# Where the low parts of a decoder step's weight blocks are made: all on VectorE instead of mostly on GpSimd

## What is computed

```
def mixer_layer(x, ...):                       # twice (DEPTH = 2)
    h = rmsnorm(x, norm_pre)
    p = h @ w_in                               # 1024 x 3840: 30 blocks of 128 columns
    rq, rk, rv, rg, sq, sk, sv, sg, ca, cb, cg = split(p)
    o_r = head_groupnorm(retention(rope(rq), rope(rk), rv)) * silu(rg)
    o_s = stickbreak(sq, sk, sv) * silu(sg)    # z -> log_sigmoid -> cumulative sum -> weights -> @ v
    o_c = conv_module(ca, cb) * silu(cg)       # gate, 31-tap depthwise conv, layernorm, swish, matmul
    y = concat([o_r, o_s, o_c]) @ w_out        # 1024 x 1024: 8 blocks, loaded again for each chunk
    return x + rmsnorm(y, norm_post)
```

## Time and profile before

| | |
|---|---|
| median of 3 runs | 1452.54 us (1452.2 to 1453.28) |
| the profiled execution | 1451.64 us, of which the profile's span is 1449.8 |
| PE busy | 1382.0 us, 95% |
| DVE busy | 891.5 us, 61% |
| ACT busy | 764.6 us, 53% |
| POOL busy | 530.4 us, 37% |
| mean granted TensorE clock | 0.983 of 2.4 GHz |

### The profile page before, as it was taken

The page is one execution under the profiler, slowest core; times in us unless marked ns, Lnnn a source line. Parts: engine busy times, 40 slices in busy tenths (PEclk is TensorE's granted clock), DMA queues, the critical chain, the costliest instruction groups (busy, mean ns, idle before and its releaser), DMA issues.

```text
span 1449.8 us, 22660 instructions
## 1 busy us (share of the span) xinstructions
PE 1382.0 (95%) x8328; PEld 1176.3 (81%) x8328; DVE 891.5 (61%) x1378; ACT 764.6 (53%) x1517; POOL 530.4 (37%) x446
## 2 busy tenths in 40 slices
PE   6999899999999999999999999998999999999996
PEld 4888678778778878899978886886767888789995
DVE  2528998985542455476762398999745235545665
ACT  4555442476435555576645644336754364656642
POOL 1535531444423453131234454234343145431211
PEclk9999999999999999999999999999999999999998
DMA  6212004111023110535342110231111311015353
GB/s 230 73 60 74 20 19 128 59 51 38 15 78 109 54 35 16 164 133 186 120 144 74 44 49 16 63 99 64 36 34 45 98 65 54 16 59 194 130 172 109
DMA packets 81167, 116.99 MB, mean 81 GB/s; under 512 B 17442, under 2 KB 62882, under 8 KB 80930
## 3 DMA queue, kind: packets, MB, share of 16 engines
q1 hardware_dynamic: 65794, 59.98, 13.2%
q10 hardware_dynamic: 15264, 55.58, 11.5%
HBM read 89.81 MB, written 19.23 MB: 75 GB/s over the span
## 4 chain that ended last, share of the span: by engine, by line
PE 74%; DVE 16%; issue 4%; ACT 3%; POOL 1%; DMA 0%; SPq 0%; ACTq 0%; DVEq 0%
PE ring L1051 17%; PE ring L1053 16%; PE ring L1052 16%; DVE MX L1709 6%; PE AV L1202 3%; DVE MX L1710 3%; PE Z L1166 3%; PE Z L1266 2%; DVE MX L1806 2%; PE Z L1182 1%; DVE stop_lo L1584 1%; PE ring L1088 1%; PE ring L1074 1%; PE Z L1196 1%; PE Z L1180 1%
## 5 line engine op out<-in xcount | busy, mean ns | idle before, releaser
L1051 PE MATMUL ring<-H_hi,w_hi 128*128 128x352 f32 x1824 | 608.1, 333 | 13.4 <-DVE H_lo L899 5.4
L1053 PE MATMUL ring<-H_hi,w_lo 128*128 128x352 f32 x1824 | 587.6, 322 | 0.0
L1052 PE MATMUL ring<-H_lo,w_hi 128*128 128x352 f32 x1824 | 586.9, 322 | 0.0
L1051 PEld LDWEIGHTS ring<-H_hi,w_hi 128*128 128x128 f32 x1824 | 343.5, 188 | 49.4 <-issue 21.1
L1052 PEld LDWEIGHTS ring<-H_lo,w_hi 128*128 128x128 f32 x1824 | 344.4, 189 | 4.3
L1053 PEld LDWEIGHTS ring<-H_hi,w_lo 128*128 128x128 f32 x1824 | 343.6, 188 | 0.0
L908 POOL TENSOR_TENSOR w_lo<-w_raw,w_hi 128x1024 fp32r<-128x1024 f32 x58 | 149.5, 2577 | 306.4 <-ACT w_hi L1292 306.4
L1890 POOL TENSOR_SCALAR attend<-attend 128x512 f32<-128x512 f32 (+4 forms) x144 | 180.4, 1271 | 112.8 <-ACT attend L1361 112.8
L1577 DVE SCALAR_TENSOR_TENSOR attend<-Z,vec_sb,attend 128x512 f32<-128x512 f32 (+4 forms) x144 | 84.8, 613 | 138.4 <-ACT attend L1369 137.4
L1709 DVE SCALAR_TENSOR_TENSOR MX<-MX,vec_sb 128x1023 f32<-128x1023 f32 (+14 forms) x120 | 165.6, 1380 | 2.2
L1292 ACT ACTIVATE w_hi<-w_raw 128x1024 fp32r<-128x1024 f32 x82 | 86.6, 1056 | 69.2 <-PE ring L1053 43.6
(11 more groups left out here) (164 smaller groups left out, 1901.5 us busy)
## 6 DMA issues: line engine op xcount, KB each, us to landing
w_raw<-in_w ACTq DMA_DIRECT2D x81, 512.0 KB, 3.5
state<-in_w ACTq DMA_DIRECT2D x25, 512.0 KB, 3.5
out_yT<-MX SPq DMA_DIRECT2D x12, 704.0 KB, 4.3
swapped<-raw_rot SPq DMA_DIRECT2D x144, 44.0 KB, 1.9
attend<-in_cache_k SPq DMA_DIRECT2D x96, 64.0 KB, 1.9
attend<-in_cache_v SPq DMA_DIRECT2D x96, 64.0 KB, 2.2
attend<-in_xT SPq DMA_DIRECT2D x3, 1408.0 KB, 12.4
attend<-out_yT SPq DMA_DIRECT2D x3, 1408.0 KB, 12.6
```

The costliest lines, as they stand in the source:

```text
L1051: nc.tensor.matmul(in_ring(step), a, x, start=(n_k == 0), stop=False)
L1052: nc.tensor.matmul(in_ring(step), a, y, start=False, stop=False)
L1053: last = nc.tensor.matmul(in_ring(step), b, x, start=False, stop=(n_k == KB - 1))
```

## The change

`low_by_dve` says DVE for every block, so that all 108 subtractions are DVE's and POOL has none. The planner runs again with that and gives every engine another list. In three places the planner's graph now demands the free `gate` buffer for all three chunks of a block, not only for the first; the kernel's own wait there (first chunk alone) is as before.

```diff
 def low_by_dve(i):
-    return i % LOADS == 1 or i % LOADS >= NB
+    return True
...
             elif name == "cb":
-                g.add("ACT", step, 0.47, x, before_gate((name, j)) if c == 0 else None, rank=0)
+                g.add("ACT", step, 0.47, x, before_gate((name, j)), rank=0)
...
             elif name in ("rg", "sg", "cg"):
-                a = g.add("ACT", step, 0.47, x, before_gate((name, j)) if c == 0 else None, rank=0)
+                a = g.add("ACT", step, 0.47, x, before_gate((name, j)), rank=0)
```

More of the change, by code:

```diff
@@ L406, in plan @@
             elif name == "cb":
-                g.add("ACT", step, 0.47, x, before_gate((name, j)) if c == 0 else None, rank=0)
+                g.add("ACT", step, 0.47, x, before_gate((name, j)), rank=0)
                 g.drain[step] = ACTn(*step)
             elif (name, i) == ("sg", NB - 1):
-                a = g.add("ACT", step, 0.47, x, before_gate((name, j)) if c == 0 else None, ACTn("sample_t", j), ACTn("gn_var", j, CH - 1),
+                a = g.add("ACT", step, 0.47, x, before_gate((name, j)), ACTn("sample_t", j), ACTn("gn_var", j, CH - 1),
                           DVEn("gated", "rg", j), rank=0)
```

## The result

The changed kernel takes 1440.09 us (median of 4 runs, 1435.54 to 1441.1) beside 1452.39 us of the kernel before (4 runs, 1452.2 to 1453.28). The ratio is 0.9908, with a 95% interval of 0.9887 to 0.993: 0.9% faster, about 13 us. The profiled execution took 1440.34 us, of which the span is 1438.1. The forecast was 1444.5.

The account below looks back on a forecast made before the run. PE is the busy engine, idling when DVE's `stop_lo` comes late because POOL's subtractions hold DVE. 1451.64 - 26.4 relief + 18.4 new waits = 1443.6, adjusted 0.9 to the runs' median: 1444.5 us, range 1431 to 1460.

Parts of the forecast that it names:

- Holding removed: DVE operations no longer held by POOL's subtractions: 16.8 us per conv stretch, plus four joins of about 1.8 us per layer.
- DVE's load in the conv stretches: Nine added subtractions, 11.9 us, against 16.8 us of holding: load falls 4.9 us, from 170.8 to about 166 of 182.
- rival 2: DVE stays the bound in the conv stretches; relief only 17.8 us against 18.4 of new waits: 1453 us, chance 0.12.
- Relief, 26.4 us: PE's gain in four stretches beside attention: 16.2 us of `stop_lo` waits, 3.4 other idle, 6.8 clock; bounds 17.8 to 40.8.
- clock term: Behind PE's longest waits, four 25 us windows at clock 0.93 would recover 1.7 us each, 6.8 in all.
- New waits, 18.4 us: Pairs 1 and 4, units 8 to 10 and just behind: waits of 7.5 us plus 1.7 clock per layer; bounds 0 to 26.8.
- the lower bound's case: In pairs 1 and 4, new waits cost nothing if they only replace the wait already standing there.
- The hole: Pairs 1 and 4, units 8 to 10: PE has no projection among them while ACT runs a 3.9 us sigmoid pass.
- Head-of-line wait and next load, nothing: DVE's `w_lo` waiting for ACT's `w_hi`, and the next block's load behind it: taken as nothing, bound 13 us a layer.
- Planner's edits, nothing: Three planner graph edits cost nothing, since on ACT a copy of chunk 1 or 2 stands behind chunk 0 anyway.
- rival 3: DVE's new subtractions hold POOL, whose clamp lies on attention's loop; PE loses 6 us: 1450.5 us, chance 0.08.
- rival 1: PE's new waits in pairs 1 and 4, units 7 to 11, outweigh the relief: 1461.5 us, chance 0.22.
- rival 4: Relief is complete: PE's idle time in the four stretches vanishes, 22.4 us gained, 1430 us; chance 0.12.

Follow-up runs that it names:

- run 3: Kernel before with its own lists, POOL's subtractions of input blocks from the third on cut to 32 of 1024 columns: 1416.13 us, 0.9746.
- run 5: Kernel before with its own lists, POOL's subtractions from the third input block on replaced by a full-width fill that reads nothing: 1415.84 us, 0.9751.
- run 1: Kernel before with its own lists, only the 58 subtractions moved from POOL's list to DVE's at their planned moments: 1431.16 us, 0.9866.
- run 2: Changed kernel's lists, with the 58 subtractions moved back from DVE's list to POOL's at their planned moments: 1460.0 us, 1.0066 of the kernel before.
- run 4: Changed kernel, DVE's subtractions of input blocks from the third on cut to 32 of 1024 columns: 1430.9 us, 0.9872 of the kernel before.
- run 11: Run 10 with planner rank 0 instead of 1 for the conv norm's passes and 6 instead of 3 for projections: 1414.48 us, 0.9741.
- run 10: Changed kernel with planner ranks 1.5 instead of 3 for taps and 0 instead of 1 for input blocks' subtractions: 1421.38 us, 0.9787.
- run 7: Changed kernel, three sigmoid passes per layer in pair 1 (4) made linear, without table loads: 1425.94 us, 0.9832 of the kernel before.
- run 9: Changed kernel with planner rank 1 instead of 3 for the taps, nothing left out: 1427.25 us, 0.9831 of the kernel before.

## Why the prediction came out right

It is 4.4 us off, with two terms that were both too large and stood against each other: that the total lies so near is in part luck. The six kernels that cross the two sets of lists with the three places of the subtraction give (us against before, from the ratios, each with 2 to 3 us to either side):

| lists | on POOL | on DVE | cut |
|---|---|---|---|
| of before | 0 | -19.5 | -36.9 |
| of the change | +9.6 | -13.4 | -18.6 |

**What bounds the kernel.** Right. POOL's reads hold DVE, DVE's `stop_lo` comes late, PE waits: runs 3 and 5 take the first link away in two ways, and the third is gone in both.

**Holding removed.** Mis-sized: 48 us of DVE were counted from the pieces on the chain, 77.7 were there (run 3). The chain shows only those that ended last. Where the difference lies, by line (before less run 3, us; in part these overlap in time): L1710 27.8, L1806 19.9, L1709 11.2, L1584 7.4, L1763 5.3, L1680 and L1740 5.0 each. The join alone was put at 14.4, four in each layer; layer 0 has five of more than 2 us.

**DVE's load in the conv stretches.** Taken as 4.9 us less in each, and run 1 has it so, 6.1 and 5.5 less. But the load still had a price: DVE's subtractions cost 17.4 us of the 36.9 in the old lists, and about 5 in the new. That is rival 2 in part.

**Relief, 26.4 us.** Mis-sized: the row of the table that goes from POOL to DVE gives 19.5 in the old lists and 23.0 in the new ones. Its `stop_lo` term was near the mark (16.2 of 20.3 us; run 1 loses 13.7). Its term for the other idle time, 3.4, was not: PE idles 34.0 us in the four stretches before and 19.8 in run 1, which leaves 0.5. Its clock term, 6.8, is the one that the traces bear out least: windows of 25 us between 25 and 1400 us lose 16.0 us to the lower clock before (eight stand at 0.93 and one at 0.94; the forecast counted four), 15.7 in run 1, 11.0 in run 3 and 24.2 in the changed kernel, each summed as (1 - clock) x 25.

**New waits, 18.4 us.** The walk found the right place, engine and order. Of its four waits per layer (0.9, 3.0, 1.6, 2.0) the trace has 1.42, 2.91, none in the list and 1.33: 5.7 for 7.5. What failed is the step from waits to cost. The four were added in full, and a column of the table gives 9.6 or 6.1 us for the new lists with the subtractions in place. The sum counted the waits that the lists bring and not those that they take away. PE's idle time shows both (us, both layers together, from the windows by stage of one execution each):

| | conv stretches | behind them |
|---|---|---|
| before | 22.2 | 11.7 |
| lists of the change, on POOL (run 2) | 11.6 | 24.3 |
| lists of before, on DVE (run 1) | 12.3 | 7.5 |
| lists of the change, on DVE (the changed kernel) | 9.7 | 14.8 |
| lists of before, cut (run 3) | 9.4 | 5.3 |
| lists of the change, cut (run 4) | 7.2 | 14.2 |

With the subtractions on POOL the new lists take some 10.6 us away and bring 12.5, with them on DVE 2.6 and 7.3. Of the 11.3 us of walked waits in the two layers these 7.3 are left as more idle time behind the conv stretches, so in part they stand in the place of waits that were there anyway, which was the lower bound's case. The hole's own price is some 7 us as far as run 11 against run 10 gives it, whose two ranks move other steps as well. With the subtractions cut the table has the lists 18.3 us dearer, with some 4 to either side, of which this idle time shows 6.6; where the rest lies is not settled.

**Head-of-line wait and next load, nothing.** Right for the conv stretches: DVE waits there for `w_hi` 0.9 and 1.0 us in front of L908, and PE's list has no wait for a `w_lo`.

**Planner's edits, nothing.** In time this was not measured. But the reason given was wrong: planned without the edits, PE's list is unchanged and ACT's list has the copy of chunk 1 of `sg` 0 ahead of chunk 0's and of the second conv pass, without a wait for the gate buffer. These lists need the edits.

**Signs named in advance.** L1710's maximum (1.03 us), `stop_lo` and DVE's busy time came as said. PE's idle time in 350 to 420 us is 5.8 us, not 10. The sign for rival 3 misled: ACT's ln waits for POOL 58.4 us instead of 35.7, but also 52.2 in run 4, without DVE's subtractions, 61.1 in run 2, with them on POOL, and only 39.2 in run 1, with all of them on DVE. The wait comes with the lists, not with the hold.

**The rivals.** 1: the new waits stayed below the relief, 6 to 10 us against 19 to 23. 2: true of a third of the `stop_lo` waits in the old lists. 3: at most some 4 us, open. 4: not with these lists, but run 11 went beyond its 1430 us with others.

## What to carry to other kernels

Before an operation is costed at its own duration, look for what it holds elsewhere: the same small instruction at ten times its median, ending when another engine's ends, is the sign, and an engine's busy time in a run without the suspect gives the whole sum, where the chain gives a part. After a change of assignment the order is a term of its own: time the old order with the new assignment, since here the order that came along gave back about a third of the gain, and another one nearly doubled it. And a new list takes waits away as well as bringing them: count PE's idle time stage by stage for both, before the new waits are added to the sum.

## What was not expected of the hardware

The granted clock differs between executions in stretches where the lists are the same. The changed kernel and run 7 run the same lists, and the same instructions up to the first conv pass; in the window from 150 us, PE is busy alike and the clock is 0.86 in the first (first fence) and 1.00 in the second. Both wait about 1.7 us for `kd` at 150 to 152 us; the first alone had waited for it just before as well, 0.67 us at 149:

```profile
150.00:175.00 25.00, 23.27 (x124) 18.62 (x122) 20.14 (x31) 12.04 (x26) 11.45 (x9) 0.86 0.07 23
```

```profile
150.00:175.00 25.00, 23.29 (x139) 18.47 (x139) 24.00 (x36) 13.62 (x28) 11.36 (x11) 1.00 0.07 23
```

One such fall is 0.14 x 25 = 3.5 us, more than the 0.2% that timing can tell. It is the same between executions of one kernel: the five of run 9 go from 1423.53 us at a mean clock of 0.988 to 1433.42 at 0.978. So a clock term that is read from one profiled execution, as in the forecast, is uncertain by a few us, and of the 11 us of run 7 some 3 are waiting, while how much of the rest the shorter passes brought can't be told from these traces.
